# A transformer kernel in three blocks: the norms' VectorE work one block ahead of ScalarE, two modulations and the first weight splits of two stages moved into the stage in front, and a new order and new places for the expert stage's loads

## The reference, cut to what matters

```python
def rmsnorm(x, g):
    xf = x.astype(jnp.float32)
    y = xf * lax.rsqrt(jnp.mean(xf * xf, axis=-1, keepdims=True) + EPS)
    return (y * g.astype(jnp.float32)).astype(x.dtype)
...
sh1, sc1, gt1, sh2, sc2, gt2 = [a[:, None, :] for a in jnp.split(c_act @ ada_w[l] + ada_b[l], 6, axis=-1)]
h = rmsnorm(x, norm1_g[l]) * (1.0 + sc1) + sh1
z = h @ w_in[l]
...
x = x + gt2 * hierarchical_moe(...)          # 4 groups of 8 experts, top 2 of one group
...
h = rmsnorm_2(x, norm_w[i]) * (1 + scale) + shift      # i = 0: GDN, i = 1: FOX
y = gdn_mixer(h, ...) or fox_mixer(h, ...)
x = x + gate * y
```

## The kernel before, in words

| load | place before | waits for | place changed | waits for |
|---|---|---|---|---|
| ex11, ex16, ex21, ex26 | | down of the expert 5 or more before, or ada | | down 7, 12, 17, 22 |
| ex31 | 5120 to 8192 | down 25, ada 18 | 12288 to 15360 | down 27, ada 20 |
| ov2 | 18432 | down 28, ada 19 | 0 | down 29, ada 21 |
| ov3 | 21504 | down 29 | 5120 | down 30, ada 21 |
| ov4 | 0 | down 32 and 30 | 20480 | down 33 |
| ov5 | 5120 | down 33 | 23552 | down 33, ada 23 |
| ov6 | 8192 | down 34 | 4096 | down 35, ada 23 |
| ov7 | 13312 | down 35 | 7168 | down 35 |
| gqk0a, gqk0b | 0, 2048 | down 36 | 0, 2048 | down 34, ada 23 |
| ba | 4096 | ada 22 | 4096 | down 38 |

## Time and profile before

### The profile page before, as it was taken

How to read it: one execution, slowest core, us unless ns; L and a number is a source line. 1 busy time by engine, 2 the same in 40 slices (tenths; PEclk the granted TensorE clock), 3 DMA queues, 4 the chain that set the end, 5 groups by cost and what they waited for, 6 DMA issues and landing times.

```text
span 1228.9 us, 20051 instructions
## 1 busy us (share of the span) xinstructions
PE 1075.5 (88%) x8110; PEld 927.7 (75%) x8110; DVE 639.8 (52%) x1382; ACT 491.7 (40%) x1100; POOL 399.1 (32%) x337
## 2 busy tenths in 40 slices
PE   2599778998999999889589989999889977999986
PEld 2596577787777777667488879899779866888866
DVE  7779965364434454334554544544453433455553
ACT  2334334502201101013376756836643534465532
POOL 0551333020000000100467564465443425555421
PEclk9699889798999999999699989999989978999987
DMA  9523351675199999963222211212211203223201
GB/s 351 206 91 142 137 179 46 255 303 216 40 417 353 397 388 406 384 253 138 103 93 89 96 70 71 104 69 105 69 69 41 99 37 138 104 103 137 104 35 35
DMA packets 25724, 198.80 MB, mean 162 GB/s; under 512 B 3104, under 2 KB 3744, under 8 KB 4512
## 3 DMA queue, kind: packets, MB, share of 16 engines
q1 hardware_dynamic: 24048, 184.77, 39.4%
q0 software_dynamic: 1152, 12.58, 2.5%
q10 hardware_dynamic: 432, 0.18, 0.1%
HBM read 196.46 MB, written 1.05 MB: 161 GB/s over the span
## 4 chain that ended last, share of the span: by engine, by line
PE 67%; DVE 18%; ACT 8%; DMA 4%; issue 3%; POOL 1%; DVEq 0%; ACTq 0%; SPq 0%
PE bank L666 65%; DVE arena L2092 6%; DVE sz L2092 3%; PE bank L670 2%; DMA ring<-in_exw 2%; DVE arena L2089 2%; DMA ring<-in_exw,small 1%; ACT wH L1489 1%; DVE hT L2092 1%; ACT arena L1489 1%; ACT xH L1486 1%; ACT arena L1486 1%; DVE xL L2092 1%; DVE arena L2095 1%; DVE wL L2089 1%
## 5 line engine op out<-in xcount | busy, mean ns | idle before, releaser
L2916 POOL TENSOR_TENSOR wL<-ring,wH 128x512 fp32r<-128x512 f32 x210 | 280.7, 1350 | 337.5 <-ACT wH L1489 337.0
L666 PE MATMUL bank<-xH,wH 128*128 128x256 f32 x800 | 252.7, 316 | 28.2 <-DVE xL L2092 24.5
L666 PE MATMUL bank<-xH,wL 128*128 128x256 f32 x800 | 233.0, 291 | 0.0
L666 PE MATMUL bank<-xL,wH 128*128 128x256 f32 x800 | 232.4, 291 | 0.0
L666 PEld LDWEIGHTS bank<-xH,wH 128*128 128x128 f32 x800 | 159.7, 200 | 44.3 <-issue 33.8
L666 PEld LDWEIGHTS bank<-xH,wL 128*128 128x128 f32 x800 | 160.4, 201 | 4.6 <-issue 4.3
L1489 ACT ACTIVATE wH<-ring 128x512 fp32r<-128x512 f32 x264 | 154.0, 619 | 20.7 <-DMA ring<-in_wts 12.3
L666 PEld LDWEIGHTS bank<-xL,wH 128*128 128x128 f32 x800 | 159.9, 200 | 0.0
L666 PE MATMUL bank<-ring,xg 128*128 128x256 f32 x640 | 148.6, 386 | 9.9 <-DMA ring<-in_exw,small 5.8
L666 PEld LDWEIGHTS bank<-ring,xg 128*128 128x128 f32 x640 | 122.0, 194 | 33.0 <-DMA ring<-in_exw,small 6.2
L2092 DVE SCALAR_TENSOR_TENSOR sz<-ring,cact,sz 128x512 f32<-128x512 f32 x168 | 134.0, 797 | 5.0 <-DMA ring<-in_wts 0.4
(11 more groups left out here) (201 smaller groups left out, 1875.7 us busy)
## 6 DMA issues: line engine op xcount, KB each, us to landing
ring<-in_wts SPq DMA_DIRECT2D x123, 1024.0 KB, 4.9
ring<-in_exw SPq DMA_DIRECT2D x32, 1536.0 KB, 9.1
ring<-in_wts SPq DMA_DIRECT2D x1, 1152.0 KB, 5.1
xT<-in_xT SPq DMA_DIRECT2D x1, 1024.0 KB, 13.7
out<-hT SPq DMA_DIRECT2D x4, 256.0 KB, 2.6
cst<-in_cst SPq DMA_DIRECT2D x1, 928.5 KB, 11.8
ring<-in_wts SPq DMA_DIRECT2D x1, 640.0 KB, 3.5
vec<-in_vec SPq DMA_DIRECT2D x1, 216.5 KB, 5.4
```

Source lines behind the costliest of these rows:

```text
L666: return pe.matmul(o, l, r, start=start, stop=stop, skip_group_check=True)
L2916: return pool.tensor_tensor(o, x, h.bitcast(F32), ALU.subtract)
```

## The change

Five edits:

1. In `normed` (VectorE) the order follows the new table AHEAD: y0, y1, l0, y2, l1, ..., y7, l6, l7, in place of y0, l0, y1, l1, ... So VectorE does y(k+1) while ScalarE does xH(k).
2. `modulation(2)` goes from behind the expert loop to u = 30 inside it; `modulation(3)` goes from the start of the third norm to before GDN's third output projection. Each now waits for the last y of the norm before.
3. The splits of gqk0a and gqk0b go into the last steps of the expert loop: ScalarE's from u = 38, VectorE's from u = 40, GpSimd's wait only for ScalarE's. The splits of fqk0b go from before the third split norm into it, one quarter behind every second block, on ScalarE, VectorE or GpSimd.
4. To let them start, the ada loads and products run faster: 8 half steps for 5 experts instead of 7 (`5 * h <= 4 * u` in chunks()), so ada 23 is done at u = 34 and not 39; ov4 and ov6 get places of their own choosing in `ring_spots()`, away from the split buffers; the first split waits, by `under_split()`, for the last expert and the last ada chunk under those buffers (down 32 and ada 22) instead of down 39 and ada 23.
5. `before(n)` no longer stops at the chunk that covers the place's start, and returns every overlapping chunk of the last 40.

```diff
--- before.py
+++ after.py
...
     h = 0
     for u in range(40):
         add(f"ex{u}" if u < 32 else f"ov{u - 32}", "expert", None, (0, 3072))
-        while h < 28 and 10 * h <= 7 * u:
+        while h < 28 and 5 * h <= 4 * u:
             j, x = 10 + h // 2, h % 2
             part = (512 * x, 512 * x + 512), (512 * (j % 6), 512 * (j % 6) + 512)
             if j < 12:
...
     out, at = {}, 0
     for name in ORDER:
         k = PLACE[name][1]
+        at = {"ov4": RING, "ov6": 4096}.get(name, at)
         if at + k > (LONG if "ex4" in out and name in WIDE else RING if name in WIDE else FIRST if "gt3b" not in out else LATE):
             at = 0
         out[name] = (at, at + k)
...
         a, b = SPOT[ORDER[m]]
         if a < hi and lo < b:
             out.append(ORDER[m])
-            if a <= lo:
-                break
     return out
 
...
                   ("own", 1), ("over", 4), ("og", 1), ("row", 8)):
     ROUTE[_name] = (_n, _k)
     _n += 2 * _k
+AHEAD = [(0, "y")] + [(k + x, n) for k in range(8) for x, n in ((1, "y"), (0, "l")) if k + x < 8]
 STEPS = ["l0", "l1", "mx", "g0", "g1", "g2", "g3", "gd", "pos", "gs", "gv", "pr0", "es0", "pr1", "es1", "em", "ed", "sum", "er", "pp",
          "v1", "a0", "a1", "a2", "a3", "pm", "v2", "b0", "b1", "b2", "b3", "o1", "vs", "vr", "fac", "wg", "wf", "own", "ow", "over",
          "og0", "og", "rows", "row", "rowi", "ws"]
...
         ada_out = sig("ada_out", range(24))
         mod_d = sig("mod_d", [(u, i) for u in G4 for i in range(3 if u == 2 else 2)])
         r2_d = sig("r2_d", range(3))
-        norm_d = sig("norm_d", [(u, k, n) for u in G4 for k in K8 for n in ("y" if u == 1 else "yl")] + [(4, k, "y") for k in K8])
+        norm_d = sig("norm_d", [(u, k, n) for u in G4 for k, n in ([(k, "y") for k in K8] if u == 1 else AHEAD)] + [(4, k, "y") for k in K8])
         norm_a = sig("norm_a", [(u, k) for u in G4 for k in K8])
         norm_h = sig("norm_h", [(u, k) for u in (0, 2, 3) for k in K8])
         hi_a = sig("hi_a", [(n, q) for n in SPLIT for q in G4])
...
         def ada_name(j):
             return f"ada{j}" if j < 12 else f"ada2_{j // 6 - 2}_{j % 6}"
 
+        def under_split():
+
+            names = [n for n in WIDE if SPOT[n][0] < RING and 12288 < SPOT[n][1]]
+            return [freed_by([n for n in names if (n[:3] == "ada") == x][-1])[0] for x in (False, True)]
+
         def used(name):
 
             x = 2 * (name[-1] == "b") + 1
...
                     turn_hid(u - 1)
                 if 2 <= u:
                     down(u - 2)
-                for _ in range((u + 1) * 7 // 5 - u * 7 // 5):
+                for _ in range((u + 1) * 8 // 5 - u * 8 // 5):
                     next(gad, None)
                 if 11 <= u and (u - 11) % 8 < 4:
                     scatter((u - 11) // 8, (u - 11) % 8)
...
                     for q in range(4):
                         e.wait_ge(loaded(name), name)
                         if name[:4] == "gqk0":
-                            e.wait_ge(dn_p, 39)
-                            e.wait_ge(ada_acc, (23, 7))
+                            for s, key in under_split():
+                                e.wait_ge(s, key)
                         if n >= 2:
                             e.wait_ge(*used(SPLIT[n - 2]))
                         c = slice(512 * q, 512 * q + 512)
...
                 for k in range(8):
                     e.wait_ge(norm_d, (u, k, "y"))
                     fn(oh[:, k, :], hT[:, k, :], ACT.Identity, bias=shift(k)).then_inc(norm_a.up((u, k)))
+                    if u == 3 and k % 2:
+                        split.go()
 
 
...
                     gather_over(u - 8)
                 if 1 <= u < 41:
                     turn_hid(u - 1)
+                if 38 <= u:
+                    split.go()
+                    split.go()
                 if 2 <= u and (u - 2) % 8 == 7:
                     high_y((u - 2) // 8)
             for k in range(8):
                 square(2, k)
-            split.need("gqk0b")
-
             exp_ln()
             root(2, 2)
             e.wait_ge(r2_d, 1)
...
             each(nx)
             each(out_proj("ao", 3, 3, True))
 
-            split.need("fqk0b")
+            split.need("fqk0a")
             root(3, 6)
             e.wait_ge(op_p, ("ao", 3, 7))
             normed(3, xH2, lambda k: adaT[:, 72 + k:73 + k])
...
 
             def modulation(u, at, out_of, *gains):
                 e.wait_ge(ada_out, out_of)
+                if u:
+                    e.wait_ge(norm_d, (u - 1, 7, "y"))
                 ts(modA[:, :], adaT[:, at:at + 8], 1.0, ALU.add).then_inc(mod_d.up((u, 0)))
                 for i, g in enumerate(gains):
                     e.wait_ge(mod_d, (u, i))
                     tt(modA[:, :], modA[:, :], g, ALU.mult).then_inc(mod_d.up((u, i + 1)))
 
             def normed(u, r, oh, ol, shift):
-                for k in range(8):
-                    stt(hT[:, k, :], xT[:, k, :], modA[:, k:k + 1], r, ALU.mult, ALU.mult).then_inc(norm_d.up((u, k, "y")))
-                    e.wait_ge(norm_a, (u, k))
-                    stt(ol[:, k, :], hT[:, k, :], shift(k), oh[:, k, :].bitcast(F32), ALU.add, ALU.subtract).then_inc(norm_d.up((u, k, "l")))
+                for k, n in AHEAD:
+                    if n == "y":
+                        stt(hT[:, k, :], xT[:, k, :], modA[:, k:k + 1], r, ALU.mult, ALU.mult).then_inc(norm_d.up((u, k, "y")))
+                    else:
+                        e.wait_ge(norm_a, (u, k))
+                        stt(ol[:, k, :], hT[:, k, :], shift(k), oh[:, k, :].bitcast(F32), ALU.add, ALU.subtract
+                            ).then_inc(norm_d.up((u, k, "l")))
+                        if u == 3 and k % 2:
+                            split.go()
 
 
...
                     gated_up(0)
                 if 1 <= u < 40:
                     gated_up(u)
-                for _ in range((u + 1) * 7 // 5 - u * 7 // 5):
+                for _ in range((u + 1) * 8 // 5 - u * 8 // 5):
                     next(gad, None)
+                if u == 30:
+                    modulation(2, 56, 15, vcol("norm_w_2", 0, 8), vcol("final_norm_g", 0, 8))
                 if 2 <= u and (u - 2) % 8 == 7:
                     low_y((u - 2) // 8)
+                if 40 <= u:
+                    for _ in range(4):
+                        split.go()
                 if 11 <= u and (u - 11) % 8 < 4:
                     scatter((u - 11) // 8, (u - 11) % 8)
             close()
             for i in range(4):
                 scatter(4, i)
-            split.need("gqk0b")
-
-            modulation(2, 56, 15, vcol("norm_w_2", 0, 8), vcol("final_norm_g", 0, 8))
             e.wait_ge(root_a, (2, 1))
             tt(rstd[:, 1, :], rstd[:, 0, :], rstd[:, 0, :], ALU.mult).then_inc(r2_d.up(0))
             e.wait_ge(r2_d, 0)
...
             nx = chain(out_proj("ao", 1, 3, 64), gates_z(3))
             weave(front(3), (back(2), 0.7), (nx, 0.95))
             each(nx)
+            modulation(3, 80, 23, vcol("norm_w_2", 8, 8))
             nx = out_proj("ao", 2, 3, 64)
             weave(back(3), (nx, 1.2))
             each(nx)
             each(out_proj("ao", 3, 3, 64, True))
 
-            split.need("fqk0b")
-            modulation(3, 80, 23, vcol("norm_w_2", 8, 8))
+            split.need("fqk0a")
             e.wait_ge(mod_d, (3, 1))
             e.wait_ge(root_a, (3, 1))
             e.wait_ge(norm_h, (2, 7))
...
                 for k in range(8):
                     e.wait_ge(norm_d, (u, k, "l"))
                     pool.tensor_scalar(hT[:, k, :], hT[:, k, :], shift(k), None, ALU.add).then_inc(norm_h.up((u, k)))
+                    if u == 3 and k % 2:
+                        split.go()
 
             def gates():
                 for j in range(4):
...
             each(nx)
             each(out_proj("ao", 3))
 
-            split.need("fqk0b")
+            split.need("fqk0a")
             normed(3, lambda k: adaT[:, 72 + k:73 + k])
             each(fox_project(0))
             for g in range(4):
```

## The result

The change made the kernel slower: medians 1247.29 us (7 runs, 1242.87 to 1251.36) against 1233.5 (7 runs, 1225.34 to 1238.71), a ratio of 1.0109 with a 95% interval of 1.0072 to 1.0146. The profiled execution has a span of 1245.5 us, 16.6 over that of before, at a mean clock of 0.926. The forecast of 1236.9 had the sign right and less than half of the size, and the time lies over the range's end of 1246.

What follows compares the result with a forecast made beforehand. The expert stage was taken to run at PE's pace with little room in the transfers. The terms +16 - 4.7 - 1.8 - 1 - 2.3 = +6.2 us on 1230.71 gave 1236.9 us, range 1228 to 1246.

Steps and rivals of the forecast that it cites:

- part 1: Expert stage: two edits change when loads may start, so it gets longer by 16 us, bounds +4 and +22.
- Part 1(a): Expert stage: denser ada loads make every fifth expert's load wait for an earlier down; +3.5 us, bounds 0 and +5.3.
- (b): Expert stage: ex31 may start only after down(27), a step later, and meets the same crowd; +4 us, bounds 0 and 6.
- (c): Expert stage: ov4 waits for down(33) instead of down(32), so PE waits 6.4 us for 4.83; +1.6, bounds -1 and +4.
- (d): Expert stage: ov6 waits for down(35) instead of down(34); +5.4 us of wait and +1.5 of slow clock, bounds +3 and +8.
- Part 2: Experts to second norm: early splits and modulation hide under the last experts; first hT 4.7 us earlier, bounds -5.5 and -2.
- Part 3: Three norms: VectorE's blocks take 1.2 us, not 1.46, taking turns with GpSimd; -1.8, -1 and -2.3 us.
- 4: Norms: GpSimd's whole addition locks VectorE out, blocks of 1.75 us; 1246 us, chance 0.10.
- 3: Expert stage: transfers become the bound, needing 405 GB/s against 389; the stage grows by 22, 1243 us, chance 0.18.
- 1: Norms: VectorE and GpSimd take no turns, blocks of 0.82 us; 5 us better, 1232 us, chance 0.12.
- 2: Expert stage: late loads ov4 and ov6 stay covered and PE waits for neither; 1224 us, chance 0.10.
- 5: Norms: VectorE keeps the port, GpSimd's additions and splits pile up, decays and forget gates wait; 1239 us, chance 0.10.

Runs made afterwards that it cites:

- e2: The changed kernel with 12 load semaphores instead of 8: 1237.73 us, 1.0022 of the kernel before.
- e8: The changed kernel, same pace, with 10 load and 6 overflow semaphores, e3's places, VectorE's bank copy earlier, ov0 and ov1 issued later: 1217.48 us, 0.9849 of before.
- e12: e4 plus a semaphore per overflow expert, VectorE's bank copy ahead in steps 8 and 9, ov0 and ov1 issued after down(27) and down(28): 1210.0 us, 0.9825 of before.
- e3: The changed kernel with other ring places for ov4 to ov7, so ov4 waits for down(32) and ov6 for down(34): 1238.05 us, 1.0041 of before.
- e5: The kernel before with only VectorE's new order (AHEAD) in the three split norms: 1222.16 us, 0.9889 of before.
- e4: The changed kernel with the old pace of 7 ada half steps per 5 experts and the old load places save ov7: 1217.23 us, 0.9878 of before.
- e6: The changed kernel with GpSimd's shift addition in the norms cut from 256 to 8 columns: 1253.5 us, 1.0139 of before.

## Why the prediction was wrong

For part 1, the expert stage, I had +16 with bounds of +4 and +22, and it grew by 30.2. **Part 1(a) is the step that failed**: +3.5 with an upper bound of 5.3, measured +14.7. The mechanism that I named is there, as the waits at ex6 (I had written ex5), ex11, ex16, ex20, ex21 and ex26, but it cost 6.9 us, 7.5 with the steps right behind: steps 5, 10, 15 and 25 lost 1.0 to 1.9 and not 0.7. In the trace of the change an expert's load that is issued first in its moment takes 6.4 to 7.0 us, and one issued right behind it about 10. As large a part, 4.0 and 4.2 in the steps 4 and 9 less the 1.1 of before, I had not seen at all: the pace also moves VectorE's copy out of bank 7, and with it when PE gets the bank. Its sign stood in the trace of before, a wait of 0.82 us for adaT in step 8, and I looked at loads only. I moved a generator's half steps and followed its DMAs; I did not follow its last step, a copy that somebody waits for. My upper bound was a bound for bandwidth, not for the stage (and its step is 0.27 us, not 0.25, which makes it 5.7).

**(b)** ex31: +4, measured +4.2. The size was right, the reason half so, and that is luck: e2 took the semaphore wait away and 2.0 us came back; e8 at the new pace and e12 at the old one issued ov0 and ov1 later, and ex31 was not waited for.

**(c)** ov4: +1.6, measured +3.6; the wait was 7.65 us where I had 6.4, and the slow clock cost 3.2 us, not the 1.5 of before. **(d)** ov6: +6.9, measured +7.6. The sum held, but e3 shows that the place was not the whole reason: with the new pace ov6 is late by 5 us even when it may start with down(34), since gqk0a and gqk0b start with it. In the change itself ov6 started at 576.1, 6 us behind them, and took its 7.0. I had taken gqk's new wait for down(34) from the table and costed it at nothing. ov2 and ov3 at nothing was right: 16.8 for 16.7.

**Part 2**: -4.7, measured -6.5, of which 1.5 came in e5 too, where none of it was moved; the edit's own part is about -5.0. The short operations behind the sums of squares took 3.4 us, and I had 3.3 (seven at 0.45 are 3.2). But it is paid by the pace: e4 has the early splits without the pace and gets nothing (29.4 against 29.2 in e5). I had said what covers the splits, and not that VectorE's products would be beside them if ada 23 were late.

**Part 3** was too small. The block was to be 1.2 us and was 1.01, since an addition costs VectorE 0.21 and not 0.37. For the three norms I had -5.1. By places: the first norm's gain, the last xL 7.5 us behind the first hT and not 11.3, was lost at once, as its bound allowed. VectorE and GpSimd in the taps behind it, and what PE waits for:

```profile
77.62 6.29 DVE L2100 SCALAR_TENSOR_TENSOR arena<-arena,vec 128x256 f32<-128x256 f32 x8
83.84 1.74 DVE L2097 TENSOR_TENSOR wL<-ring,wH 128x512 fp32r<-128x512 f32 x1
```

```profile
79.41 5.62 POOL L2933 TENSOR_TENSOR wL<-ring,wH 128x512 fp32r<-128x512 f32 x4 [3.12 <-ACT wH L1494]
```

```profile
85.64 0.58 PE L671 MATMUL bank<-xH,wH 128*128 128x256 f32 x1 [5.09 <-DVE wL L2097]
```

Eight taps took 6.29 us and the split behind them 1.74. Before, the taps took 3.25 us and the split behind them 0.68:

```profile
83.33 0.68 DVE L2089 TENSOR_TENSOR wL<-ring,wH 128x512 fp32r<-128x512 f32 x1
```

PE waited 5.09 us for that split, 0.97 before. It had been 2.4 us ahead of the kernel before on the same matmul at the norm's end (54.47 for 56.91) and was 3.0 behind at 88.80 (85.83). VectorE lost nothing in all: with the eight taps that follow, 7.36 us before and 3.25 now, its stretch is 11.1 us in both. Only the split that PE wants comes later in it. From the second norm's first hT on, the change won 6.3 us and e5 7.5, against 3.3 forecast. In the third norm the splits of fqk0b cost what their move saved: e4 comes to the third norm 4.9 us sooner than e5 and loses 4.3 behind it, 1.6 of it inside (the last xL 9.13 us behind the first hT, not 7.51), as these rows of the change show:

```profile
1039.05 0.47 DVE L2100 SCALAR_TENSOR_TENSOR xL<-hT,adaT,xH 128x256 fp32r<-128x256 f32 x1
1039.45 1.50 DVE L2100 SCALAR_TENSOR_TENSOR hT<-xT,modA,rstd 128x256 f32<-128x256 f32 x1
1040.87 0.69 DVE L2100 SCALAR_TENSOR_TENSOR xL<-hT,adaT,xH 128x256 fp32r<-128x256 f32 x1
```

```profile
1039.27 1.39 POOL L2933 TENSOR_TENSOR wL<-ring,wH 128x512 fp32r<-128x512 f32 x1
```

**The rivals.** 4 and 3 gave 1246 and 1243, the numbers nearest to 1247.3, and both for a reason that the runs refute. 3, the transfers, falls by e2 and e8. 1, no turns, has the wrong mechanism (e6) though the norms' gain is nearer to its 10 us. 4, the whole addition, fell: the pitch is 1.01, not 1.75. The Trainium skill (SBUF — State Buffer, "SBUF: two separate sides") has the two engines exclude each other for a whole instruction; the addition that ran beside VectorE cost it 0.21 us of its 1.03, and the measurement decides. For the splits of two inputs the rule and the rows come near each other: a split costs VectorE 1.05 us (e6) and takes 1.39 in the row above. 2 and 5 fell too: ov4 and ov6 were waited for, and GpSimd ended 2.8 us earlier than before, not later. None of the rivals had a wait that the pace makes on another engine's copy, and the slow side of my range ended 1.3 us under the median.

## What to carry to other kernels

When a change alters how many steps of a side job go into each turn of a loop, follow the side job's last step as well as its loads: which bank or buffer it frees, what now stands ahead of it in its queue, and who asks for it in that turn. A small wait in the trace (0.82 us here) is a place where two schedules already touch. And separate the edits before they are judged together: here the new order alone is worth -1.1% (7.5 us of it seen in the norms' stretches), the pace that was to make room for 5 us of early splits costs 1.8%.
